# Experts in split fp32r with rings apart, and weighted rows scattered by token and choice

## The reference

```python
def routed_experts(h, idx, wts, w_gate, w_up, w_down):   # idx, wts: two experts for each token
    ...                                  # rows sorted by expert, each expert padded to blocks of 128 rows
    def one_group(args):
        xg, e = args
        return (jax.nn.silu(xg @ w_gate[e]) * (xg @ w_up[e])) @ w_down[e]
    yb = lax.map(one_group, (xb, block_expert)).reshape(rows, d)
    y_sorted = yb[dest] * wts.reshape(-1)[order][:, None].astype(h.dtype)
    return jax.ops.segment_sum(y_sorted, tok_sorted, num_segments=n)
```

## Time and profile before

| what | us |
|---|---|
| median of 3 runs (lowest, highest) | 2308.5 (2307.08, 2308.64) |
| profiled execution, its own time | 2307.37 |
| span of its trace | 2305.9 |
| `list_blocks`, from its first issue | from 1555.9 |
| `experts`, first transposes of gathered rows | from 1585.05 |
| last evictions of the experts | 2172.6 |
| `combine`, from its first issue to the end of the span | 2178.3 to 2305.9 |

### The profile page before, as it was taken

How to read it: one execution, slowest core, us unless ns; L and a number is a source line. 1 busy time by engine, 2 the same in 40 slices (tenths; PEclk the granted TensorE clock), 3 DMA queues, 4 the chain that set the end, 5 groups by cost and what they waited for, 6 DMA issues and landing times. The chain is left out here.

```text
span 2305.9 us, 28759 instructions
## 1 busy us (share of the span) xinstructions
PE 1992.8 (86%) x9169; PEld 1423.8 (62%) x9170; DVE 879.8 (38%) x1859; ACT 514.6 (22%) x1114; POOL 264.2 (11%) x406
## 2 busy tenths in 40 slices
PE   5699999999689999992999999954999999999600
PEld 2588888888567777762888888732444444444300
DVE  3466666666230000014355555542111111111188
ACT  2244444444030000003111111100111111111111
POOL 0000000000000000000001110011111111111165
PEclk9799999999699999996999999976999999999855
DMA  8322122222185454527344334307998454879486
GB/s 277 119 94 77 75 91 84 93 93 83 45 302 201 163 204 163 204 62 248 136 146 156 135 136 146 100 26 236 336 388 297 152 203 148 308 260 368 180 304 236
DMA packets 185655, 407.95 MB, mean 177 GB/s; under 512 B 27774, under 2 KB 107134, under 8 KB 180610
## 3 DMA queue, kind: packets, MB, share of 16 engines
q1 hardware_dynamic: 157540, 312.26, 39.0%
q0 software_dynamic: 20880, 69.03, 8.2%
q10 hardware_dynamic: 7200, 26.22, 2.8%
HBM read 296.47 MB, written 110.99 MB: 177 GB/s over the span
## 5 line engine op out<-in xcount | busy, mean ns | idle before, releaser
L1982 PE MATMUL ex<-expert_ring,gathered_T 128*128 x816 | 361.1, 596 | 4.2 <-SPq L1818 2.9
L1982 PEld LDWEIGHTS ex<-expert_ring,gathered_T 128*128 128x128 f32 x816 | 151.8, 191 | 177.3 <-issue 177.3
L265 PE MATMUL mix<-w_mix_hi,hT_hi 128*128 128x512 f32 (+3 forms) x544 | 204.4, 376 | 3.9 <-DVE hT_lo L645 2.6
L267 PE MATMUL mix<-w_mix_lo,hT_hi 128*128 128x512 f32 (+3 forms) x544 | 198.8, 365 | 0.0
L266 PE MATMUL mix<-w_mix_hi,hT_lo 128*128 128x512 f32 (+3 forms) x544 | 198.4, 365 | 0.0
L2003 PE MATMUL ex<-expert_ring,hidden_T 128*128 x400 | 179.9, 592 | 0.0
L1933 DVE SCALAR_TENSOR_TENSOR silu_e<-tanh_e,ex 128x256 f32<-128x256 f32 x51 | 21.5, 421 | 352.5 <-ACT tanh_e L1888 352.5
L1155 DVE SCALAR_TENSOR_TENSOR ma_rows<-tanh_rows,ga 128x512 f32<-128x512 f32 (+1 forms) x34 | 21.8, 683 | 337.0 <-PE ga L267 186.6
L265 PE MATMUL gb<-w_b_hi,h_parts_b 128*128 128x512 f32 (+1 forms) x272 | 109.2, 401 | 27.8 <-DVE w_b_lo L1450 18.6
L265 PE MATMUL ga<-w_a_hi,h_parts 128*128 128x512 f32 (+1 forms) x272 | 109.2, 401 | 17.3 <-DVE w_a_lo L1140 14.7
L2003 PEld LDWEIGHTS ex<-expert_ring,hidden_T 128*128 128x128 f32 x400 | 72.1, 190 | 71.7 <-issue 71.7
(11 more groups left out here) (302 smaller groups left out, 3279.0 us busy)
## 6 DMA issues: line engine op xcount, KB each, us to landing
expert_ring<-in_w_gate SPq DMA_DIRECT2D x32, 1024.0 KB, 8.8
expert_ring<-in_w_up SPq DMA_DIRECT2D x32, 1024.0 KB, 12.4
expert_ring<-in_w_down SPq DMA_DIRECT2D x32, 1024.0 KB, 14.3
expert_rows<-y_block ACTq DMA_DIRECT2D x50, 512.0 KB
h_parts<-hT_split SPq DMA_DIRECT2D x16, 1024.0 KB, 5.1
mixer_parts<-oT_split SPq DMA_DIRECT2D x32, 512.0 KB, 8.3
w_ada_part<-in_w_ada SPq DMA_DIRECT2D x16, 1024.0 KB, 10.8
h_parts_b<-hT_split SPq DMA_DIRECT2D x16, 1024.0 KB, 4.9
```

The costliest lines, as they stand in the source:

```text
L265: nc_mm(out, left[0], right[0], start=first, stop=False)
L267: return nc_mm(out, left[0], right[1], start=False, stop=last)
L1982: last = nc.tensor.matmul(ps[2 + par][:, :], xT[par][:, k, :], w[:, bass.ds(slot * WC + k * 2 * EH, 2 * EH)], start=(k == 0), stop=(k == K ...
```

## The change

Each block's turned rows and its gate/up weights are now split into hi and lo: ACT rounds, DVE subtracts (`turned`, `weights`), and PE adds three fp32r products where there was one of fp32. The down product stays fp32. The split weights are two buffers of their own, written two blocks ahead. Because the ring is read only by the split, SP gives a gate/up slot back when the split of the expert's last block is done; down weights have their own slots, given back after the down product, and their own signal. SP now issues the gate/up load of expert n, and then the down load of expert n-2.

The table holds three words per slot: the token, 2 x token + choice, and the weight. Empty slots hold 4160, which is beyond both tensors, so a gather or scatter passes over them. ACT multiplies a block's rows by their weights as it evicts them, and POOL scatters them to row 2 x token + choice of `weighted_rows`. There each token's two rows are neighbours: in `combine`, ACT loads a tile of pairs by a plain transfer, and DVE adds them. The fill of unused rows, the index arithmetic in `list_blocks` and three kept tensors are gone.

```diff
@@ program @@
-            "table": dram("slot_tokens", (TABLE, 1), I32),
+            "table": dram("slot_records", (TABLE, 3), I32),
             "blocks": dram("block_list", (4, P), I32),
             "cum": dram("block_ends", (1, NE), I32),
-            "ys": dram("expert_rows", (MAX_BLOCKS * P, D)),
+            "y2": dram("weighted_rows", (2 * TOKENS, D)),
...
@@ sweep_gate_b @@
-            pool.dma_start(s["table"].rearrange("(p c) o -> p (c o)", p=P), zero).then_inc(filled, 16)
-            pool.wait_ge(filled, 16)
+            pool.wait_ge(setup, 5)
+            table = s["table"].rearrange("(p n c) f -> p n (c f)", p=P, n=2)
+            for n in range(2):
+                pool.dma_start(table[:, n, :], empty).then_inc(filled, 16)
+            pool.wait_ge(filled, 32)
...
+                step(nc.vector.tensor_copy(rec[0:m, :, 0], idf[0:m, :].to_broadcast([m, 2])))
+                step(nc.vector.scalar_tensor_tensor(out=rec[0:m, :, 1], in0=idf[0:m, :].to_broadcast([m, 2]), scalar=2.0,
+                                                    in1=small[0:m, 36:38], op0=ALU.mult, op1=ALU.add))
+                step(nc.vector.tensor_copy(rec[0:m, :, 2].bitcast(F32), r[0:m, 118:120]))
...
@@ instead of load_expert @@
+GU = KD * 2 * EH
+DOWN = 2 * D
+
+
+def load_gate_up(sp, a, ring, e, slot, done):
+
+    ww = ring[:, slot * GU:(slot + 1) * GU].rearrange("p (k c) -> p k c", k=KD)
+    one = lambda t: t[0, bass.ds(e, 1), :, :].rearrange("o (k p) h -> p (o k) h", p=P)
+    sp.dma_start(ww[:, :, 0:EH], one(a["w_gate"])).then_inc(done, 16)
+    sp.dma_start(ww[:, :, EH:], one(a["w_up"])).then_inc(done, 16)
+
+
+def load_down(sp, a, ring, e, slot, done):
+
+    ww = ring[:, RING * GU + slot * DOWN:RING * GU + (slot + 1) * DOWN].rearrange("p (k c) -> p k c", k=2)
+    sp.dma_start(ww, a["w_down"][0, bass.ds(e, 1), :, :].rearrange("o (k p) d -> p (o k) d", p=P)).then_inc(done, 16)
...
@@ list_blocks @@
-            step(nc.vector.tensor_tensor(eq[:, :, :], small[:, 0:NE].unsqueeze(1).to_broadcast([P, NK, NE]),
-                                         eid.unsqueeze(2).to_broadcast([P, NK, NE]), ALU.is_equal))
-            step(nc.vector.tensor_tensor(eq[:, :, :], eq[:, :, :], starts[:, :].unsqueeze(1).to_broadcast([P, NK, NE]), ALU.mult))
-            step(nc.vector.tensor_reduce(ys[:, :], eq[:, :, :], AX_X, ALU.add))
-            step(nc.vector.scalar_tensor_tensor(out=ys[:, :], in0=ys[:, :], scalar=float(P), in1=kept["rank"][:, :, :].rearrange("p t k -> p (t k)"),
-                                                op0=ALU.mult, op1=ALU.add))
-            step(nc.vector.tensor_copy(kept["yrow"][:, :, :].rearrange("p t k -> p (t k)"), ys[:, :]))
-
...
@@ experts, sync @@
             def arrived(slot, times):
-                sp.wait_ge(w_in[slot], times * 48)
+                sp.wait_ge(w_in[slot], times * 32)
...
+            def next_down(n, older):
+                wait_apart(sp, down, last_block(n - RING - 2), passed)
+                load_down(sp, a, w, n - 2, older, d_in[older])
+
+            def expert(g, slot, first=False):
+
+                n, older = g * RING + slot, (slot - 2) % RING
+                arrived(older, g + slot // (RING - 1))
+                if not first or slot >= 2:
+                    down_arrived(slot, g if slot else g - 1)
+                wait_apart(sp, w_lo, last_block(n - RING) * 2, passed)
+                load_gate_up(sp, a, w, n, slot, w_in[slot])
+                if not first or slot >= 2:
+                    next_down(n, older)
+
+            for slot in range(RING):
+                expert(1, slot, first=True)
+            with sp.Fori(2, NE // RING) as g:
                 for slot in range(RING):
-
-                    arrived((slot + 2) % RING, g + slot // (RING - 1))
-                    last = sp.value_load(ends[0:1, bass.ds(g * RING + slot - RING, 1)], min_val=1, max_val=MAX_BLOCKS)
-                    wait_apart(sp, down, last, passed)
-                    load_expert(sp, a, w, g * RING + slot, slot, w_in[slot])
-                    unused(g * (-RING) + (PAIRS + RING - 1 - slot), total)
-            for slot in range(RING - 2, RING):
-                arrived(slot, NE // RING)
-            sp.wait_ge(filled, (PAIRS - RING) * 16)
+                    expert(g, slot)
...
@@ experts, gpsimd @@
-                                        in_offset=bass.IndirectOffsetOnAxis(ap=idx[:, par:par + 1].bitcast(U32), axis=0)).then_inc(x_in[par], 16)
+                                        in_offset=bass.IndirectOffsetOnAxis(ap=idx[:, par, 0:1].bitcast(U32), axis=0),
+                                        bounds_check=TOKENS - 1, oob_is_err=False).then_inc(x_in[par], 16)
+            def records(b, slot, before):
+
+                if before is not None:
+                    wait_apart(pool, stored[slot % 2], before, passed)
+                row = listed(pool, 2, b)
+                pool.dma_start(rec[:, slot, :], s["table"][bass.ds(row, P), 1:3]).then_inc(rec_in[slot], 16)
+
+            def scatter(b, slot):
+                wait_apart(pool, y_out, b + 1, passed)
+                pool.indirect_dma_start(out=s["y2"], out_offset=bass.IndirectOffsetOnAxis(ap=rec[:, slot, 0:1].bitcast(U32), axis=0),
+                                        in_=y[:, slot % 2, :], in_offset=None,
+                                        bounds_check=2 * TOKENS - 1, oob_is_err=False).then_inc(stored[slot % 2], 16)
+
+            def step(b, slot, n, before):
+                gather(b + 2, slot % 2, n)
+                records(b + 1, (slot + 1) % 4, before)
+                scatter(b - 1, (slot - 1) % 4)
...
@@ experts, scalar @@
-                nc.scalar.copy(xT[par][:, 0:4, :], ps[0][:, :].rearrange("p (k m) -> p k m", m=P)).then_inc(xT_a, 1)
+                if not isinstance(b, int) or b > 1:
+                    act.wait_ge(gu, b - 1)
+                for n in range(2):
+                    last = nc.scalar.copy(xT[par][0][:, 4 * n:4 * n + 4, :], ps[n][:, :].rearrange("p (k m) -> p k m", m=P))
+                last.then_inc(xT_hi, 1)
+
+            def weights(b, par):
+                need, slot = listed(act, 1, b), listed(act, 0, b)
+                act.wait_ge(w_ready, need)
+                if not isinstance(b, int) or b > 1:
+                    act.wait_ge(gu, b - 1)
+                for n in range(2):
+                    nc.scalar.copy(wg[par][0][:, n * HG:(n + 1) * HG], w[:, bass.ds(slot * GU + n * HG, HG)]).then_inc(w_hi, 1)
 
...
-            def store(b, par, before):
+            def weigh(b, slot, landed, before):
                 act.wait_ge(down, b + 1)
                 if before is not None:
-                    act.wait_ge(stored[par], before)
-                nc.scalar.copy(y[:, par, 0:512], ps[5][:, :]).then_inc(y_a, 1)
-                act.wait_ge(y_a, b + 1)
-                act.wait_ge(y_d, b + 1)
-                act.dma_start(s["ys"][bass.ds(b * P, P), :], y[:, par, :]).then_inc(stored[par], 16)
-
+                    act.wait_ge(stored[slot % 2], before)
+                act.wait_ge(rec_in[slot], landed)
+                for n in range(2):
+                    last = nc.scalar.activation(y[:, slot % 2, n * 512:(n + 1) * 512], ps[5 + n][:, :], ACT.Copy, scale=weight(slot))
+                last.then_inc(y_out, 1)
...
+            def step(b, slot, landed, before):
+                par = slot % 2
                 hidden(b - 1, 1 - par)
                 silu(b, par)
                 turned(b + 1, 1 - par)
-                store(b - 1, 1 - par, before)
...
+                weights(b + 2, par)
+                weigh(b - 1, (slot - 1) % 4, landed, before)
...
@@ experts, vector @@
-                dve.wait_ge(x_turned, b + 1)
-                nc.vector.tensor_copy(xT[par][:, 4:8, :], ps[1][:, :].rearrange("p (k m) -> p k m", m=P)).then_inc(xT_d, 1)
+                dve.wait_ge(xT_hi, b + 1)
+                for n in range(2):
+                    last = nc.vector.tensor_tensor(xT[par][1][:, 4 * n:4 * n + 4, :], ps[n][:, :].rearrange("p (k m) -> p k m", m=P),
+                                                   xT[par][0][:, 4 * n:4 * n + 4, :].bitcast(F32), ALU.subtract)
+                last.then_inc(xT_lo, 1)
+
+            def weights(b, par):
+                slot = listed(dve, 0, b)
+                for n in range(2):
+                    at = slice(n * HG, (n + 1) * HG)
+                    dve.wait_ge(w_hi, b * 2 + 1 + n)
+                    nc.vector.tensor_tensor(wg[par][1][:, at], w[:, bass.ds(slot * GU + n * HG, HG)], wg[par][0][:, at].bitcast(F32),
+                                            ALU.subtract).then_inc(w_lo, 1)
 
...
@@ experts, tensor @@
-                need, slot = listed(pe, 1, b), listed(pe, 0, b)
-                pe.wait_ge(w_ready, need)
-                pe.wait_ge(xT_a, b + 1)
-                pe.wait_ge(xT_d, b + 1)
+                pe.wait_ge(w_lo, b * 2 + 2)
+                pe.wait_ge(xT_lo, b + 1)
                 if not isinstance(b, int) or b > 1:
```

(22 more changed lines are left out.)

223 lines of the change are left out of this document (108 added, 115 removed).

## The result

Over four runs each on the same chip the changed kernel took 2338.25 us (2330.41 to 2343.1), the kernel before 2307.9 (2307.08 to 2308.64): a ratio of 1.0128, 95% interval 1.0099 to 1.0158. It is slower; 2258 us with a range of 2234 to 2300 was forecast. The profiled execution took 2330.41 us, its span is 2329.0.

The account below looks back on a forecast made before the run. Experts were taken as bound by PE, combine by DVE with DMA close behind; span 2305.9 - 67 + 16 + 9 + 3.5 + 1 - 12 = 2256.4 us, given as 2258 us, range 2234 to 2300.

Parts of the forecast that it names:

- Gate and up: Expert stage, PE: 24 fp32r matmuls 0.229 us apart cut the block period from 11.39 to 10.02 us, -67 us.
- The chain on POOL: Expert stage: scatter, next list and gather delay PE's transposes, period 10.35 instead of 10.02 us, +16 us.
- rival C: Expert stage: skipping rows saves nothing and POOL is the bound, period 11.53, +58 us, 2316 us; chance 0.10.
- my own formula: POOL's chain: two steps take at least 8.8 + L + 0.85 + G, with L scatter and G gather, issue to landing.
- The row at hand: Earlier trace: a list issued at 1581.36 behind a gather was there 0.84 us after that gather's rows let PE start.
- What hides beside it: Expert stage, per 10.02 us: ACT's work of 7.0 us and DVE's of 6.7 both fit beside PE.
- Rings: Gate/up weights needed two steps earlier, slots returned about three steps earlier, so SP's queue gains more than it owes.
- Start: Start of the expert stage: block 1 waits for ACT's and DVE's split, block 2 comes later, +9 us.
- End: Last scatter of the expert stage: POOL's start and issue and a slower landing than ACT's store, +3.5 us.
- Last stage: Combine: DVE loses copy, scaling and 0.06 us per tile, DMA bytes limit the gain, -12 us.
- table: Start of the last mixer sweep: the three times larger token table adds 0.58 MB beside weight loads, +1 us.

Follow-up runs that it names:

- split_only: The kernel before with only the fp32r split of gate/up and the separate rings, without scatter and records: 2248.3 us, ratio 0.9751.
- store_in_order: The changed kernel with POOL's scatter replaced by a plain store of the 512 KB in block order, same queue: 2329.1 us, ratio 1.0092.
- list_on_act: The changed kernel with the list of block b+2 loaded from ACT's queue, after weighting block b-2: 2241.9 us, ratio 0.9716.
- list_ahead: The changed kernel with POOL loading block b+3's list right after issuing block b+2's gather, into one of four slots: 2252.6 us, ratio 0.9766.

## Why the prediction was wrong

**Gate and up: right.** Matmul starts lie 0.227 us apart, and where nothing waits the period is 10.0:

```profile
2177.71 1.03 PE L2042 MATMUL ex<-identity,gathered 128*128 128x128 f32 x8
...
2187.72 1.03 PE L2042 MATMUL ex<-identity,gathered 128*128 128x128 f32 x8
```

The -67 us were there to be had; split_only got 59 on the clock.

**The chain on POOL is the step that failed.** The prediction gave it +16 us, a period of 10.35. Measured: 11.91, that is 49 x (11.91 - 10.02) = 93, and PE's transposes waited 135 us, over the 60 that I had named as the sign of rival C. Two errors are in it. The size: I let the gather start 0.85 behind the landing of a scatter of 5.1, 5.95 us after the scatter's issue; at 1709.47 to 1718.31 it was 8.8. That scatter took 6.9 us to land (6.1 in the median), its list 1.0 more, and POOL started 0.9 after that. With that and a gather of 4.6, my own formula gives (8.8 + 8.8 + 4.6) / 2 = 11.1. The form: I counted only the chain of two steps that goes through PE and divided by two. Beside it runs the one-step loop list, gather, records, scatter, list on POOL alone, which no prefetch on PE's side can relax: 11.1 us where nothing stretches it, more with the stretched gathers. The two take turns, and the mean is above either; 0.24 us of the difference are the stretched instructions, the rest was not taken apart.

The belief under the first error was that a list is slow only by what stands ahead of it in its own queue. The row at hand fitted that, and in the changed kernel every list did land just behind its scatter; what I had too short was the scatter itself under the weights' traffic, and what I had left out was that this traffic holds up a list with nothing ahead of it too. The earlier trace rows gave lists of 0.5 KB a median of 4.8 us and 2.2 at the least, with only gathers in the queue, which should have warned me. Rival C named the right mechanism, POOL as the bound, with a period of 11.53 and 2316 us; it got 0.10.

**What hides beside it: right.** ACT's casts took 1899 ns (1.93 forecast), DVE's low parts 2289 (2.31) and 686 (0.6), and none of them stands between PE's blocks. DVE's share in it that I set to nothing, holding up POOL, was 0.37 us an instruction and about 19 us in all.

**Rings: 0 forecast, and right as a net.** The weights are needed two steps earlier and the gate/up slots come back earlier, and the forecast let the second pay for the first. The run without the early return shows the size of it, 33 us, which the forecast had not given.

**Start: +9 forecast, +6.8 measured. End: +3.5 forecast, +11.5 measured.** The last weighting stands behind ACT's casts for blocks that do not exist:

```profile
2200.43 3.70 ACT L1939 CAST gate_up_hi<-expert_ring 128x2048 fp32r x2 [0.56 <-issue]
...
2204.03 1.26 ACT L1955 ACTIVATE y_block<-ex,row_records 128x512 f32<-128x512 f32 x2
2206.24 1.63 POOL L1892 DMA_INDIRECT weighted_rows<-y_block,row_records  x1 [3.33 <-ACT y_block L1955]
2219.45 0.34 SPq L2122 DMA_DIRECT2D x_c<-x_after_mixers  x1
```

and from the scatter's start to the next stage are 13.2 us, where ACT's store at 2173.51 was followed by it at 2178.29, 4.8 us. It is not the scatter that takes so long. By the view of its line it landed in 3.2 us, at 2209.5; then POOL's DRAIN, the instruction that stands in its queue ahead of the barrier, took 9.0 us, in which the DMA engines moved nothing (window 2209.6 to 2218.5: share 0.00). The scatter's landing and the DRAIN, and last the DRAIN of the kernel before:

```profile
DMA to landing us min/median/max: 3.2/3.2/3.2
...
L1772 POOLq DRAIN  x1: 8971/8971/8971, 2209.6 to 2209.6; - x1
...
L1779 POOLq DRAIN  x1: 8562/8562/8562, 2155.0 to 2155.0; - x1
```

Before, POOL had nothing left to issue at 2155 and its DRAIN hid behind PE's last products; now POOL is the last engine of the stage, and 8.4 of the 11.5 us are its end laid bare. The other 3.1 are the later weighting and POOL's start. The forecast had a slower landing there and no DRAIN. It is as long behind the plain store of store_in_order (9.0) and 4.3 in list_on_act and the kernels built on it, where POOL issues no lists: 4.7 of the 10.7 us by which list_on_act beats list_ahead. What the DRAIN waits for, no run shows.

**Last stage: -12 forecast, -18.0 measured.** I held it to 359 GB/s; the DMA engines moved 405 (window 2260 to 2280), and DVE's four operations of some 1.22 us gave 4.9 us a tile. The last constant came 21.2 us in, 5.9 later than before (15.3), where I had put 3.

Sum of the misses on the span: start and period 71.6, end 8.0, last stage -6.0, table about -1; together the 72.6 between 2256.4 and 2329.0.

## What to carry to other kernels

Before adding work to a queue that already runs ahead of the bottleneck, write down every cycle in it, also those that close within one engine's program, and compare each with the new period, not with the old one. A small load that the next instruction waits for is dear wherever large loads are in flight, so issue it a step ahead; moving it to another queue did not make it quicker here. Look also at which engine is last in a stage: an end that hid before can come to lie bare. Two edits that are each neutral or good alone can cost 4% together, when one makes the bottleneck fast enough to expose what the other made long.

## What the runs showed of the hardware

- A load of 1.5 KB landed in 3.0 us (median) with an eighth of the weight traffic and in 5.9, at most 7.6, with all of it; 1.9 at the least. From ACT's queue, with nothing large ahead of it, it was not seen to land sooner (gathers that waited for it started 5.8 to 7.3 us after its issue). From POOL's, it never landed before the scatter ahead of it.
- POOL's DRAIN at the end of the expert stage took 9.0 us behind a loop with lists, gathers, records and scatters, 8.6 with lists and gathers, 4.3 without lists; nothing moved on the DMA engines meanwhile in the changed kernel.
- DVE instructions with two operands in SBUF lengthened POOL's indirect DMA instructions (1053 to 1426 ns, at most 3061), not its plain ones (564).
- In the last stage the 16 DMA engines moved 405 and 422 GB/s at a share of 1.01 and 1.02 in the changed kernel, and between 377 (list_on_act) and 424 (list_ahead) at the same shares in later ones, above the 359 at which the expert stage of the kernel before stood at 1.01.
- fp32r matmuls of 512 columns issued 0.227 us apart also from weights that ACT and DVE had written two blocks before, three for 0.68 us, where the fp32 product took 0.86.
